# The last two experts' tokens finished in the layout of their slots and scattered over the stored output

## The reference

```python
# x: residual rows, (544, 1024); 16 experts, 2 of them for each token
for e in range(N_EXPERTS):
    h = silu(xt @ w_gate[e]) * (xt @ w_up[e])
    y = y + combine[:, e:e + 1] * (h @ w_down[e])
x = x + y
# final norm, for prompt rows and for sample rows
y_prompt = xp * rsqrt(mean(xp * xp) + EPS) * final_norm_g
y_sample = xs * rsqrt(mean(xs * xs) + EPS) * final_norm_g
```

## Time and profile before

| | us |
|---|---|
| median of 3 runs | 725.1 |
| lowest and highest | 722.34, 727.65 |
| the profiled execution's own time | 726.61 |
| its span, first to last instruction | 724.9 |
| PE busy | 668.2 (92%) |
| DVE, ACT, POOL busy | 261.0, 183.6, 143.5 |

### The profile page before, as it was taken

One profiled execution on the slowest core, in us unless ns is written; L12 is line 12 of the kernel. 1 busy time (PEld: TensorE's weight loads), 2 busy tenths in 40 slices (PEclk: granted clock), 3 DMA queues, 4 the chain that ended last, 5 costly groups with the idle time before them and its releaser, 6 DMA issues.

```text
span 724.9 us, 14801 instructions
## 1 busy us (share of the span) xinstructions
PE 668.2 (92%) x5460; PEld 428.3 (59%) x5460; DVE 261.0 (36%) x817; ACT 183.6 (25%) x460; POOL 143.5 (20%) x227
## 2 busy tenths in 40 slices
PE   4999999999998888998999977999999999899796
PEld 2476497847646465557555565866685856455342
DVE  4157220137435657765243574112111011111117
ACT  3110212203132973675331211011111010101105
POOL 0405007130143187400000202011211112020000
PEclk9999999999999999999999977999999999999999
DMA  9995238063479176503496247999999999999963
GB/s 346 368 328 187 69 126 292 26 210 117 136 246 357 40 217 173 178 1 118 151 429 262 84 175 276 404 384 389 379 371 404 359 386 375 370 390 384 356 246 127
DMA packets 56785, 185.60 MB, mean 256 GB/s; under 512 B 9021, under 2 KB 30814, under 8 KB 50562
## 3 DMA queue, kind: packets, MB, share of 16 engines
q1 hardware_dynamic: 44914, 152.54, 55.8%
q0 software_dynamic: 11792, 32.05, 14.5%
HBM read 172.57 MB, written 13.93 MB: 257 GB/s over the span
## 4 chain that ended last, share of the span: by engine, by line
PE 73%; DMA 10%; DVE 6%; SPq 5%; ACT 3%; issue 2%; DVEq 0%; POOLq 0%; ACTq 0%
PE ps L690 67%; DMA ring<-in_w_down_dram 6%; SPq L467 4%; PE ps L937 2%; DMA ring<-in_cmp_pages_dram 1%; PE ps L1207 1%; DMA ring<-in_w_out_dram 1%; DMA ring<-in_w_in_dram 1%; SPq L427 1%; PE ps L964 1%; DMA ugr<-h_rows,qbd 1%; ACT tabs L1648 1%; PE ps L840 0%; PE ps L784 0%; DVE tabs L2051 0%
## 5 line engine op out<-in xcount | busy, mean ns | idle before, releaser
L690 PE MATMUL ps<-ring,xr 128*128 128x512 f32 (+3 forms) x640 | 138.8, 414 | 9.6 <-DMA ring<-in_w_in_dram 9.6
L690 PEld LDWEIGHTS ps<-ring,xr 128*128 128x128 f32 (+1 forms) x640 | 68.4, 151 | 72.1 <-issue 58.8
L690 PE MATMUL ps<-ring,vnr 128*32 128x128 f32 (+1 forms) x1152 | 78.6, 325 | 1.8 <-DMA ring<-in_w_gate_dram 1.2
L690 PE MATMUL ps<-ring,work 128*32 128x128 f32 (+2 forms) x512 | 72.4, 372 | 2.2 <-DMA ring<-in_w_out_dram 1.6
L690 PEld LDWEIGHTS ps<-ring,vnr 128*32 128x32 f32 (+1 forms) x1152 | 54.3, 123 | 26.1 <-issue 9.4
L427 POOL DMA_DIRECT2D ring<-in_sel_pages_dram x96 | 51.4, 536 | 90.5 <-issue 57.0
L690 PE MATMUL ps<-ring,qT 128*32 128x256 f32 (+2 forms) x320 | 56.2, 513 | 5.9 <-DMA ring<-in_w_down_dram 5.3
L2814 POOL DMA_INDIRECT x_rows<-kvn,qbd x14 | 20.5, 1466 | 202.5 <-DVE kvn L2582 62.7
L690 PE MATMUL ps<-ring 128*128 128x128 f32 (+1 forms) x512 | 59.6, 279 | 0.5 <-DMA ring<-in_cmp_pages_dram 0.5
L690 PEld LDWEIGHTS ps<-ring 128*128 128x128 f32 x512 | 58.8, 191 | 0.9 <-DMA ring<-in_cmp_pages_dram 0.6
L2532 DVE COPY vnr<-ps 128x256 f32<-128x256 f32 (+3 forms) x16 | 8.1, 508 | 140.8 <-PE ps L1207 140.8
(11 more groups left out here) (401 smaller groups left out, 821.0 us busy)
## 6 DMA issues: line engine op xcount, KB each, us to landing
ring<-in_w_gate_dram SPq DMA_DIRECT2D x11, 2048.0 KB, 25.8
ring<-in_w_down_dram SPq DMA_DIRECT2D x10, 2048.0 KB, 33.3
ring<-in_w_up_dram SPq DMA_DIRECT2D x9, 2048.0 KB, 27.1
xr<-in_w_gate_dram SPq DMA_DIRECT2D x5, 2048.0 KB, 32.4
tabs<-in_w_up_dram SPq DMA_DIRECT2D x5, 2048.0 KB, 35.2
ring<-in_cmp_pages_dram SPq DMA_DIRECT2D x64, 128.0 KB, 5.3
ring<-in_cmp_pages_dram POOLq DMA_DIRECT2D x64, 128.0 KB, 5.3
ring<-in_w_in_dram SPq DMA_DIRECT2D x3, 2048.0 KB, 9.0
```

The source lines that it names most:

```text
L690: return nc.tensor.matmul(out, lhsT, rhs, start=start, stop=stop)
```

## The change

The residual rows of the last two experts' slots are gathered from DRAM by POOL into `x3_slots`, one row for each of the 128 slots. PE adds to them, in PSUM, `same_token` times `y_last`, where `same_token` (128x128) says which two slots hold the same token, so that a token that has both experts gets both terms in both of its slots. ACT and DVE root and norm this as a sixth tile, into `out_slots`. The five tiles are rooted and normed as loaded, without these experts, and stored. Then POOL, once all five stores have landed, scatters the 128 rows over the output: one indirect DMA for the prompt's output and one for the samples'; a slot whose token isn't in that output has an index past its bound, and nothing is written for it.

The matrix is made early: DVE copies the slots' token numbers and makes the indices for the samples (`last_slot_columns`, after expert 0's products), PE transposes the numbers spread over 128 columns, and DVE compares (`same_tokens`, in the turn of expert 1).

```diff
@@ block.sync
-            for i in NORM_ORDER[0:TILES - 1]:
-                sp.wait_ge(sem("out_ready"), NORMED[i] + 1)
+            for i in range(TILES):
+                sp.wait_ge(sem("out_ready"), i + 1)
                 dst = o[0][i * P:(i + 1) * P, :] if i < PT else o[1]
                 sp.dma_start(dst, x2[0:ROWS[i], i, :]).then_inc(sem("stored"), 16)
-            i = NORM_ORDER[TILES - 1]
-            for n in range(2):
-                sp.wait_ge(sem("out_ready"), TILES + n)
-                sp.dma_start(o[0][i * P:(i + 1) * P, W * n:W * n + W], x2[:, i, W * n:W * n + W]).then_inc(sem("stored"), 16)
-            sp.wait_ge(sem("stored"), 16 * (TILES + 1))
@@ block.tensor
             turn_of(2)
             last_of(0)
+            te.wait_ge(sem("last_rows"), 1)
+            nc.tensor.transpose(pb[7][:, 384:512], slot_wide, ident).then_inc(sem("spread_mm"), 1)
...
+                if n == 2:
+                    te.wait_ge(sem("last_rows"), 2)
                 last_of(n - 1)
...
+            def last_rows_summed():
+
+                te.wait_ge(sem("x3_slots_in"), 16)
+                for n in range(2):
+                    mm(pb[n], ident, x3_slots[:, W * n:W * n + W], True, False)
+                for n in range(2):
+                    te.wait_ge(sem("y_out%d" % n), E)
+                for n in range(2):
+                    mm(pb[n], same_token, y_last[:, W * n:W * n + W], False, True).then_inc(sem("spread_mm"), 1)
@@ block.scalar
+            def root_of_squares(k, rows, src):
+
+                A(ring[0:rows, 2 + k // 4, D * (k % 4):D * (k % 4) + D].rearrange("p (n w) -> p n w", n=2), src, ACT.Square,
+                  accum_out=small[0:rows, 2 * k:2 * k + 1]).then_inc(sem("x3_sq"), 1)
+                act.wait_ge(sem("x3_sq"), k + 1)
+                A(small[:, 32 + k:33 + k], small[:, 2 * k:2 * k + 1], ACT.Sqrt, bias=small[:, 16:17], scale=1.0 / D
+                  ).then_inc(sem("rstd"), 1)
+
+            def tile_root(i):
+                act.wait_ge(sem("x3_in%d" % min(i, 3)), 16 if i < 3 else 32)
+                root_of_squares(i, ROWS[i], x2[0:ROWS[i], i, :].rearrange("p (n w) -> p n w", n=2))
...
+            with act.If(more == 0):
                 A(small[:, 159:160], cst[:, C_ONE:C_ONE + 1], ACT.Sqrt)
+                for i in range(3):
+                    tile_root(i)
+                y_out(E - 1)
+                for i in range(3, TILES):
+                    tile_root(i)
+                last_slots_root()
@@ block.vector
             with dve.If(more == 0):
-                sums_and_norms()
+                dve.wait_ge(sem("vectors_in"), 80)
+                for i in range(3):
+                    last_norm(i)
+                y_out(E - 1)
+                for i in range(3, TILES):
+                    last_norm(i)
+                last_slots_norm()
@@ block.gpsimd
+            def last_rows_gathered():
+
+                po.wait_ge(sem("last_rows"), 2)
+                po.indirect_dma_start(x3_slots, None, scratch_x3, bass.IndirectOffsetOnAxis(last_slot_i.bitcast(U32), 0),
+                                      bounds_check=last_token, oob_is_err=False).then_inc(sem("x3_slots_in"), 16)
+
             with po.If(more == 0):
                 po.wait_ge(sem("y_added"), 16 * (E - 2))
                 po.sem_inc(sem("y_all"), 1)
+                po.wait_ge(sem("xt_mm"), E - 1)
+                last_rows_gathered()
...
+            po.wait_ge(sem("stored"), 16 * TILES)
+            po.wait_ge(sem("out_ready"), TILES + 2)
+            for dst, rows, at in ((o[0], SEQ, last_slot_i), (o[1], NS, last_sample_i)):
+                po.indirect_dma_start(dst, bass.IndirectOffsetOnAxis(at.bitcast(U32), 0), out_slots, None,
+                                      bounds_check=last_of_output[rows], oob_is_err=False).then_inc(sem("x3_slots_in"), 16)
+            po.wait_ge(sem("x3_slots_in"), 16 * 3)
```

More of the change, by code:

```diff
@@ L340, in hybrid_layer @@
         expert_at = ints[:, 32:32 + E - FIXED]
[L341 to L345, removed]
         gf = [buf[:, PT * W:TILES * W] for buf in (ugr, vnr)]
         y_last = tabs[:, 1024:2048]
-        token_row = work[:, 0:TOK]
-        rows_of_last = cst[:, C_SL:C_SL + TOK]
+        same_token = cst[:, C_SL:C_SL + P]
+        x3_slots = ugr[:, 0:D]
+        out_slots = vnr[:, 0:D]
         down_slots = ([ring[:, 0, D * f:D * f + D] for f in range(FE)], [ring[:, 1, D * f:D * f + D] for f in range(FE)],
@@ L353, in hybrid_layer @@
         DOWN_LOADS = (16, 16, 16 * FE)
-        token_row_i = kwT[:, :].bitcast(I32)
-        last_slot = kwT[:, 0:1]
+        slot_wide = kwT[:, 0:P]
+        last_slot, last_sample, before_samples = (kwT[:, 400 + k:401 + k] for k in range(3))
+        last_slot_i, last_sample_i = ints[:, 60:61], ints[:, 61:62]
         def adds_to(n):
@@ L1456, in _ @@
             last_of(E - 1)
[L1458 to L1480, removed]
+            def last_rows_summed():
[6 more added lines that the diff above has]
+                    mm(pb[n], same_token, y_last[:, W * n:W * n + W], False, True).then_inc(sem("spread_mm"), 1)
             with te.If(more == 0):
-                last_experts_spread()
+                last_rows_summed()
             with te.Else():
@@ L1868, in _ @@
             more = act.value_load(ints[0:1, 80:81], min_val=0, max_val=1)
-            y_out(E - 1)
-            def squares_and_roots():
-                A(small[:, 159:160], cst[:, C_ONE:C_ONE + 1], ACT.Sqrt)
[L1875 to L1890, removed]
@@ L1892, in _ @@
-            with act.If(more == 0):
-                squares_and_roots()
+            def root_of_squares(k, rows, src):
[4 more added lines that the diff above has]
+                  ).then_inc(sem("rstd"), 1)
@@ L2592, in y_out, with last_slot_columns, same_tokens @@
                                 ).then_inc(sem("y_out1"), 1)
[L2594 to L2602, removed]
+            def last_slot_columns():
+                for k, n in ((0, E - 1), (1, E - 2)):
+                    part = slice(LIGHT_CAP * k, LIGHT_CAP * k + LIGHT_CAP)
+                    V.tensor_copy(last_slot_i[part, :], slot_tokens[0:LIGHT_CAP, n:n + 1])
+                    ins = V.tensor_copy(last_slot[part, :], slot_tokens[0:LIGHT_CAP, n:n + 1])
+                link(ins)
+                link(V.tensor_scalar(last_sample, last_slot, -float(SEQ), None, ALU.add))
+                link(V.tensor_scalar(before_samples, last_sample, 0.0, float(FAR), ALU.is_lt, ALU.mult))
+                link(V.tensor_tensor(last_sample, last_sample, before_samples, ALU.add))
+                link(V.tensor_copy(last_sample_i, last_sample))
+                V.tensor_copy(slot_wide, last_slot.to_broadcast([P, P])).then_inc(sem("last_rows"), 1)
+            def same_tokens():
+                dve.wait_ge(sem("spread_mm"), 1)
+                V.tensor_scalar(same_token, pb[7][:, 384:512], last_slot, None, ALU.is_equal).then_inc(sem("last_rows"), 1)
                 dve.wait_ge(sem("last_rows"), 2)
+                link(V.memset(small[:, 0:16], 1.0))
+                link(V.memset(small[:, 16:17], EPS))
             def experts(b):
@@ L2616, in experts @@
                         dve.wait_ge(sem("slots_ready"), 3)
+                        last_slot_columns()
                     if n > E * b:
@@ L2621, in experts @@
                     if n == 1:
-                        last_expert_rows()
+                        same_tokens()
                 y_out(E * b + E - 2)
@@ L2629, in _, with scaled_by_root @@
             more = dve.value_load(ints[0:1, 80:81], min_val=0, max_val=1)
[L2630 to L2646, removed]
+            def scaled_by_root(k, rows, src, dst, ready):
+                dve.wait_ge(sem("rstd"), 5 + TILES + k)
+                rs = small[0:rows, 32 + k:33 + k]
+                link(V.reciprocal(small[:, 32 + k:33 + k], small[:, 32 + k:33 + k]))
+                for n in range(2):
+                    ins = V.scalar_tensor_tensor(out=dst[n], in0=src[n], scalar=rs, in1=gf[n][0:rows, :],
+                                                 op0=ALU.mult, op1=ALU.mult)
+                    if n >= 2 - ready:
+                        ins.then_inc(sem("out_ready"), 1)
@@ L2648, in last_norm @@
             def last_norm(i):
                 rows = ROWS[i]
[L2650 to L2674, removed]
-                summed(4, 0)
-                last_norm(0)
-                summed(4, 1)
-                last_norm(1)
-                last_norm(2)
-                last_norm(4)
-                last_norm(3)
+                halves = [x2[0:rows, i, W * n:W * n + W] for n in range(2)]
@@ L2683, in _, with last_slots_norm @@
+                scaled_by_root(i, rows, halves, halves, 1)
+            def last_slots_norm():
+                scaled_by_root(TILES, P, pb, [out_slots[:, W * n:W * n + W] for n in range(2)], 2)
             steps = chain[0]
             with dve.If(more == 0):
-                sums_and_norms()
+                dve.wait_ge(sem("vectors_in"), 80)
```

(10 more changed lines are left out.)

4 lines of the change are left out of this document (added).

## The result

| | median | runs | profiled execution: own time, span |
|---|---|---|---|
| before | 723.81 us | 4 (722.34 to 727.65) | 726.61, 724.9 us |
| after | 734.32 us | 4 (732.60 to 734.91) | 734.91, 733.2 us |

The ratio of the times is 1.0139, with a 95% interval of 1.0106 to 1.0173: the changed kernel is slower by about 10 us (7.7 to 12.5). Forecast were 2.8 us faster, and a range that ends at 727.2.

The account below looks back on a forecast made before the run. The weight stream was taken to decide until about 679.6, then a tail of 18.2 us from 706.7. Ten spreads give back some 11, tile 2's wait takes 3.3, an indirect write about 5: 722.3 us, range 719.4 to 727.2.

Parts of the forecast that it names:

- the last of the sum: At the program's end: 0.4 us from the last landing to the span's end, kept as before, giving 722.1.
- rival B: At the scatters: an indirect write costs what the indirect add does, 8.0 us to landing; 726.9 us in all; chance 0.14.
- D: Something no row shows, above all in the expert stage or the second scatter: either sign, to about 729; chance 0.08.
- the prediction's own signs of being wrong: Scatters landing under 3 or over 6 us, tile 2 pushed beyond 707.6 or absent at 706.7, weight stream's end moving from 679.6.
- C: At the tile loads: what the new gather takes from tile 2's load, taken as 0.7 us between 0 and 1.3.
- The new wait for tile 2: On ACT and DVE: the last expert's output stands behind tile 2's landing, root and norm, costing 3.3 us.
- The gather: On POOL's queue: up to 128 rows, 0.52 MB, asked for near 697.6 and in before PE needs them.
- The scatters: At the end on POOL: two indirect writes issued at 716.5 and 717.8, the second landing 3.9 us after issue.
- The early parts: Small DVE and PE instructions that make the matrix early, under the cover of the weight stream: cost nothing.
- Rival C: At the tail's start: tiles 0 to 2 come earlier, so the reordering does not bite; 720.5 us; chance 0.06.
- The base: Starting time from which the 2.8 us gain was taken off: the median of 725.1 us.

Follow-up runs that it names:

- run 1: Changed kernel with the block's closing drain left out on POOL: 723.47 us, ratio 0.9989 to the kernel before.
- run 2: Kernel before with the same closing drain on POOL left out: 722.78 us, ratio 0.9985 to the kernel before.
- run 3: Kernel before with POOL also waiting at its end for the six stores, so its closing drain comes last: 733.22 us, ratio 1.0138.
- Run 8: Changed kernel without POOL's closing drain, last expert's y_out moved ahead of tile 2's root and norm: 722.82 us, ratio 0.9991 to the kernel before.
- run 7: Kernel before with the change's early DVE and PE instructions added to no use: 725.56 us, ratio 1.0010 to the kernel before.

## Why the prediction was wrong

The step that failed is the last of the sum: "Between the last landing and the span's end lie 0.4 us now, and I keep that: 722.1." Those 0.4 us are what lies between SP's last landing and the end. For a kernel that ends on POOL they are 9.3, of which 8.9 are POOL's closing drain. The row was there to be read, hidden beside the old tail at 701.2. I read busy time, waits, the timeline, the DMAs and the chain, and this drain is in none of them. Nor did rival B find it: it asked what a scatter costs until it lands, not what POOL does after it. D, "something that no row shows", was wrongly named, since a row showed it, and it ended at 729. Slower by over 1% had a chance of 0.05, and it came. Runs 1 to 3 are the proof: away with the drain, and the slowdown goes; delay it in the old kernel, and the same slowdown comes.

Two of the prediction's own signs of being wrong came, but neither made the kernel slower: the second scatter landed in under 3 us, and the weight stream's end moved in this trace.

In the trace of after, with 3.5 us taken off for the later end of the weight stream, the other steps stand so:

| step | forecast | trace of after, less 3.5 |
|---|---|---|
| C, what tile 2's load pays | 0.7 | 8.39 against 7.86: 0.5 |
| both halves of y_out done | 710.8 | 710.6 |
| PE's last product ends | 712.7 | 712.7 |
| slots' norm ends | 715.8 | 715.8 |
| tile 4 stored | 716.4 | 716.3 |
| first scatter | 716.5 | 716.7 |
| second scatter | 717.8 | 718.0 |
| its landing after issue | 3.9 | 2.42 |
| last landing | 721.7 | 720.4 |
| end | 722.1 | 729.7 |

That the steps up to the issue of the scatters agree within 0.2 us is partly luck: from the first tile load to the first scatter this trace took 19.2 us, others up to 23.0.

- *The new wait for tile 2.* Right in place and size in this trace: ACT's square of tile 2 has [0.50 <-DMA xr<-x_rows] before it at 710.21, and DVE's half of y_out ends at 714.12. Run 8 shows no gain from taking tile 2 out of it, since DVE's own row of work stands right behind it.
- *The gather.* "Asked for near 697.6 and should be in" was loose: it landed 8.6 us after its issue, and PE waited 0.54 for it, which cost nothing under the wait until y_out.
- *C.* After against before gives 0.5, run 1 against run 2 gives 8.55 - 7.8 = 0.7. By the round robin of the Trainium skill ("DMA: Bandwidth & Descriptors", section "Queues, rings and completion order") it would have been nearly 1.3 by the prediction's estimate. That estimate took the gather for 0.52 MB; the trace shows 0.38 MB on POOL's queue while it runs, so at 400 GB/s the most that the loads could pay is 0.95. The two pairs show 0.5 and 0.7, but landings differ by more than that between traces without a gather, so they don't settle it.
- *The scatters.* Between plain store and gather, nearer the store: 3.29 and 2.42, not 3.9, and far from rival B's 8.0. The Trainium skill's estimate of 3.2 (same page, section "Anatomy of one DMA - SWDGE (gpsimd) path") came nearer for the first, but it was worked out for 0.52 MB; both scatters together moved 0.38, for which the same formula gives an estimate of 2.9. The second, whose landing ends the work, took 1.5 us less than the sum had; it can write 32 rows at most.
- *The early parts.* Nothing that shows, as forecast (run 7, within 1.2 us faster and 2.6 slower).
- *Rival C.* Tiles 0 to 2 didn't come early enough in any trace.
- *The base.* The difference was taken off 725.1, the median of three runs. 29 runs of each later session give 724.93 and 723.88.

Without the drain the forecast would have been 2.8 us faster, and run 1 measured 0.8 faster, with an interval that ends at 2.5: too good by about 2 us. Every number came from a single trace in which the tiles landed quickly, which fits that, but isn't shown to be the cause.

## What to carry to other kernels

Before moving the last work of a program to another engine, look up how each engine closes: the row of its drain at the block's end, which stands in neither the busy time nor the timeline nor, at the end, in the chain, and which is free only while another engine ends later. If a kernel must end on POOL, put a drain into an idle stretch of POOL that follows its bulk of DMAs: that took the closing one from 8.9 to 0.2 us, at no cost that could be measured. The stretch has to be long: the added drains took 10.0 to 15.0 us here. And where a change lets work start at a landing that had slack so far, the spread of that landing can become part of the time; one trace gives one draw of it.

## What the runs showed of the hardware

- POOL's closing drain grows with what POOL did since its last one, told here by its DMAs: 0.21 us behind 2, 0.38 behind 4, 3.41 behind 41, 8.65 behind 217, 8.89 behind 220. It doesn't shrink while POOL waits: 8.646 us at 701.2 and 8.646 at 720.8. ACT's and DVE's closing drains took 0.06 to 0.08 us in after. Drains that began with DMAs of POOL under way took 10.0 to 15.0.
- Plain indirect writes with lists of 128 places for rows of 4 KB, from SBUF (the core's on-chip memory) to DRAM, landed 3.3 us (prompt rows) and 2.4 us (at most 32 rows) after their issue on a quiet queue, 0.38 MB in all; the indirect gather of such rows, 0.38 MB, took 8.6 beside the tile loads.
